# S5 mixer on one Trainium2 core: paired states for the carried product, wider products for u, one more factor in the FFN

## What is computed

```python
S5_GROUP, S5_GROUPS, S5_STATE = 16, 64, 64

def _s5_direction(u, lam_re, lam_im, log_dt, b_re, b_im, c_re, c_im, reverse):
    lam = lax.complex(lam_re, lam_im)
    dt = jnp.exp(log_dt)[:, None]
    lam_bar = jnp.exp(lam * dt)
    b_bar = ((lam_bar - 1.0) / lam)[..., None] * lax.complex(b_re, b_im)
    bu = einsum('bsgp,gnp->bsgn', u, b_bar)            # complex
    # h[t] = lam_bar * h[t-1] + bu[t], forwards or backwards over the 256 tokens
    _, hs = lax.associative_scan(combine, (a, bu), axis=1, reverse=reverse)
    return einsum('gpn,bsgn->bsgp', lax.complex(c_re, c_im), hs).real

def s5_mixer(h, ..., d_skip, w_glu):
    u = h.reshape(b, s, S5_GROUPS, S5_GROUP)
    y = (y_fwd + y_bwd).reshape(b, s, d) + d_skip * h
    g = jax.nn.gelu(y)
    val, gate = jnp.split(g @ w_glu, 2, axis=-1)
    return val * jax.nn.sigmoid(gate)
```

## Time and profile before

| what | us |
|---|---|
| median of 3 runs | 2703.33 (2701.67 to 2703.73) |
| the profiled execution | 2698.23, with a span of 2696.4 |
| PE busy | 2579.1, 96% of the span |
| DVE busy | 1822.7, 68% |
| ACT busy | 1242.6, 46% |
| POOL busy | 241.6, 9% |
| mean granted clock of PE | 0.973 |

### The profile page before, as it was taken

The page is one execution under the profiler, slowest core; times in us unless marked ns, Lnnn a source line. Parts: engine busy times, 40 slices in busy tenths (PEclk is TensorE's granted clock), DMA queues, the critical chain, the costliest instruction groups (busy, mean ns, idle before and its releaser), DMA issues.

```text
span 2696.4 us, 54054 instructions
## 1 busy us (share of the span) xinstructions
PE 2579.1 (96%) x22954; PEld 2507.2 (93%) x22954; DVE 1822.7 (68%) x2288; ACT 1242.6 (46%) x1442; POOL 241.6 (9%) x276
## 2 busy tenths in 40 slices
PE   7999849999999989999999999999999999999998
PEld 7999748999999979999999998999999999999998
DVE  5887865656566657556557557976557557986655
ACT  5334404334566644335334336575334334665433
POOL 5300140002000000000000000510000000330000
PEclk9999858999999999999999999999999999999999
DMA  5553004554676745553554554434555554443453
GB/s 205 190 186 106 18 18 157 188 187 158 187 165 151 162 93 197 187 178 140 184 184 178 187 187 151 148 127 160 190 184 185 187 187 150 158 148 141 174 187 123
DMA packets 65837, 430.73 MB, mean 160 GB/s; under 512 B 8288, under 2 KB 11360, under 8 KB 15904
## 3 DMA queue, kind: packets, MB, share of 16 engines
q1 hardware_dynamic: 58864, 410.30, 41.9%
q0 software_dynamic: 6000, 17.46, 5.2%
q10 hardware_dynamic: 832, 0.92, 0.1%
HBM read 426.45 MB, written 1.15 MB: 159 GB/s over the span
## 4 chain that ended last, share of the span: by engine, by line
PE 90%; DVE 6%; ACT 2%; issue 1%; DMA 0%; DVEq 0%; ACTq 0%
PE psum L1865 26%; PE psum L1866 26%; PE psum L1867 25%; PE psum L2187 1%; PE psum L2063 1%; DVE w_lo L1271 1%; PE psum L1898 1%; ACT w_hi L818 1%; PE psum L2163 1%; PE psum L2175 1%; PE psum L2024 1%; PE psum L1967 1%; PE psum L2033 1%; PE psum L1991 1%; PE psum L2166 1%
## 5 line engine op out<-in xcount | busy, mean ns | idle before, releaser
L1865 PE MATMUL psum<-h_hi,w_hi 128*128 128x256 f32 x4320 | 1220.7, 283 | 24.7 <-DVE h_lo L1309 14.9
L1866 PE MATMUL psum<-h_lo,w_hi 128*128 128x256 f32 x4320 | 1211.2, 280 | 0.0
L1867 PE MATMUL psum<-h_hi,w_lo 128*128 128x256 f32 x4320 | 1210.9, 280 | 0.0
L818 ACT ACTIVATE w_hi<-raw 128x2048 fp32r<-128x2048 f32 x387 | 740.3, 1914 | 907.5 <-PE psum L1867 907.5
L1271 DVE TENSOR_TENSOR w_lo<-raw,w_hi 128x2048 fp32r<-128x2048 f32 x387 | 889.4, 2299 | 376.4 <-ACT w_hi L818 376.2
L1865 PEld LDWEIGHTS psum<-h_hi,w_hi 128*128 128x128 f32 x4320 | 815.7, 189 | 35.9 <-issue 28.7
L1866 PEld LDWEIGHTS psum<-h_lo,w_hi 128*128 128x128 f32 x4320 | 816.0, 189 | 1.2 <-issue 1.0
L1867 PEld LDWEIGHTS psum<-h_hi,w_lo 128*128 128x128 f32 x4320 | 814.9, 189 | 0.0
L1865 PE MATMUL psum<-act_hi,w_hi 128*128 128x256 f32 x1536 | 429.9, 280 | 1.7 <-DVE w_lo L1271 1.0
L1866 PE MATMUL psum<-act_lo,w_hi 128*128 128x256 f32 x1536 | 429.3, 279 | 0.0
L1867 PE MATMUL psum<-act_hi,w_lo 128*128 128x256 f32 x1536 | 429.1, 279 | 0.0
(11 more groups left out here) (316 smaller groups left out, 2552.9 us busy)
## 6 DMA issues: line engine op xcount, KB each, us to landing
raw<-in_panels SPq DMA_DIRECT2D x387, 1024.0 KB, 4.8
arena<-bias_by_distance POOLq DMA_DIRECT2D x32, 384.0 KB, 7.8
x<-in_x SPq DMA_DIRECT2D x1, 1024.0 KB, 5.9
arena<-in_s_cbd POOLq DMA_DIRECT2D x4, 256.0 KB, 3.2
arena<-in_s_b SPq DMA_DIRECT2D x1, 1024.0 KB, 15.4
arena<-in_s_c SPq DMA_DIRECT2D x1, 1024.0 KB, 17.2
hidden<-in_s_cbd POOLq DMA_DIRECT2D x4, 256.0 KB, 3.3
arena<-arena POOLq DMA_DIRECT2D x32, 32.0 KB, 1.9
```

The lines of the kernel that those rows point to most:

```text
L818: a.activation(w_hi[:, s, :], raw[:, s, :], ACT.Copy).then_inc(hi_ready, 1)
L1865: t.matmul(o, w[0], xin[0], start=start, stop=False, skip_group_check=True)
L1866: t.matmul(o, w[0], xin[1], start=False, stop=False, skip_group_check=True)
L1867: return t.matmul(o, w[1], xin[0], start=False, stop=stop, skip_group_check=True)
```

## The change

- `carried(n, f)` takes one matmul for a pair where it took two: all 128 rows of W, 64 outputs, and 64 columns that come from `s5.zbd`, a buffer that holds the lower group's 31 states in the lower partitions at the left and the upper group's in the upper partitions at the right, with zeros elsewhere. ACT sets the two buffers to zero once and, after the scan, fills one for every f with 4 copies of 64 partitions by 248 elements (`s5_spread`). `carried` waits for the 4 copies, and the copies of turn n wait until `carried` of turn n - 2 is done.
- `within(f)` makes two matmuls of 64 output channels where it made one of 128. `rows_of_u` takes all eight channel tiles at once, 256 columns a matmul, in half as many.
- DVE makes all of its five W ahead of the scan; POOL waits for them (`s5_w_ready`), since it now uses DVE's temporary. Tiles run through `carried` as 0, 1, 2, 3, 6, 7, 4, 5. All four copies to `s5.y` go to DVE.
- `S5_EARLY` is 6: the FFN ahead of S5 has 12 more operations of DVE. In that FFN the copy to `act_hi` goes from DVE to ACT.
- POOL makes the powers in three rounds (powers 2; 3 and 4; 5 to 8) instead of seven.

```diff
@@ places
-        s5.w = [s5_factor(v) for v in (held[2], slot[6], slot[2], slot[5], b_flat, slot[3], slot[4], held[0])]
+        s5.w = [s5_factor(v) for v in (held[2], slot[6], slot[2], held[0], b_flat, slot[3], slot[4], slot[5])]
+        s5.zbd = hidden_flat.rearrange("p (b r c n) -> p b r c n", b=2, r=2, c=NC)
-        S5_EARLY = 5
+        S5_EARLY = 6
-        W_ORDER = (0, 1, 2, 3, 4, 6, 5, 7)
+        W_ORDER = (0, 1, 2, 3, 6, 7, 4, 5)
@@ sync: panels
                     if n == s5_n0 + 3:
-                        sp.wait_ge(s5_out_ready, W_ORDER.index(7) + 1)
+                        sp.wait_ge(s5_out_ready, W_ORDER.index(3) + 1)
@@ gpsimd
-                for k in range(2, S5_T + 1):
-                    then(tt(t0, p[:, 0, k - 1], p[:, 0, 1], ALU.mult), tt(t1, p[:, 1, k - 1], p[:, 1, 1], ALU.mult),
-                         tt(t2, p[:, 0, k - 1], p[:, 1, 1], ALU.mult), tt(t3, p[:, 1, k - 1], p[:, 0, 1], ALU.mult))
-                    then(tt(p[:, 0, k], t0, t1, ALU.subtract), tt(p[:, 1, k], t2, t3, ALU.add))
+                for k in (1, 2, 4):
+                    f0, f1 = (p[:, r, k].unsqueeze(1).to_broadcast([P, k, S5_G]) for r in range(2))
+                    lo, hi = slice(1, k + 1), slice(k + 1, 2 * k + 1)
+                    then(tt(q0, p[:, 0, lo], f0, ALU.mult), tt(q1, p[:, 1, lo], f1, ALU.mult),
+                         tt(q2, p[:, 0, lo], f1, ALU.mult), tt(q3, p[:, 1, lo], f0, ALU.mult))
+                    then(tt(p[:, 0, hi], q0, q1, ALU.subtract), tt(p[:, 1, hi], q2, q3, ALU.add))
...
+                pool.wait_ge(s5_w_ready, len(W_DVE))
@@ scalar: ffn
+                def high(c, i=None):
+                    if st["s5_follows"]:
+                        a.wait_ge(act_ready, f * FFC + c + 1 if i is None else i * 2 + f * FFC + c + 1)
+                        a.activation(act_hi[:, c % 2], act[:, c % 2], ACT.Copy).then_inc(act_hi_ready, 1)
@@ scalar: s5_mixer
+                for b in range(2):
+                    a.activation(s5.zbd[:, b].rearrange("p r c n -> p (r c) n"), zeros[:, 0:2 * S5_C].bitcast(F32).unsqueeze(
+                        1).to_broadcast([P, 2 * NC, 2 * S5_C]), ACT.Copy).then_inc(s5_zeroed, 1)
...
+                a.wait_ge(s5_step, 2 + 4 * (S5_C - 2))
+                for n, f in enumerate(W_ORDER):
+                    if n >= 2:
+                        a.wait_ge(s5_out_ready, n - 1)
+                    for d in range(2):
+                        for e in range(2):
+                            half = slice(e * S5_N, (e + 1) * S5_N)
+                            z = s5.z[half, :, f * NC + 4 * d:f * NC + 4 * d + 4, :]
+                            at = e * S5_C + 1 - d
+                            a.activation(s5.zbd[half, n % 2, :, 4 * d:4 * d + 4, at:at + S5_C - 1],
+                                         z[:, :, :, 0:S5_C - 1] if d == 0 else z[:, :, :, S5_C - 2::-1],
+                                         ACT.Copy).then_inc(s5_spread, 1)
@@ vector
-                    steps(ahead, 2)
+                    steps(ahead, 3)
...
-                due = s5_v(5)
+                due = s5_w(0)
...
-                for f, k in ((1, 4), (2, 5), (6, 6)):
+                for f, k in ((1, 4), (2, 5), (6, 6), (7, 7)):
@@ tensor
-                        t.matmul(s5_y_bank(f, g % 2)[:, at:at + S5_C], s5.tc[:, g].rearrange("p i m -> p (i m)"),
+                        for up in range(2):
+                            t.matmul(s5_y_at(f, g, 1)[half[up]], s5.tc[:, g, 4 * up:4 * up + 4].rearrange("p i m -> p (i m)"),
...
-                                    for e in range(2):
-                                        z = s5.z[half[e], r, f * NC + 4 * d + pair]
-                                        last = t.matmul(s5_y_bank(f, e)[half[up], at:at + S5_C - 1],
-                                                        s5.w[f][half[e], r, 4 * d + pair, half[up]],
+                                    last = t.matmul(s5_y_at(f, 2 * pair, 2)[half[up]], s5.w[f][:, r, 4 * d + pair, half[up]],
+                                                    s5.zbd[:, n % 2, r, 4 * d + pair, :],
```

More of the change, by code:

```diff
@@ L111, in build @@
         stages = stages[:stop]
-    for st, after in zip(stages, stages[1:] + [{}]):
+    for n, (st, after) in enumerate(zip(stages, stages[1:] + [{}])):
         st["next"] = after if after.get("late") else None
+        st["s5_follows"] = [q["kind"] for q in stages[n + 1:n + 3]] == ["norm", "s5"]
     final = stages[-1]["kind"] == "final"
@@ L879, in ffn @@
                         split(p + 4, i, 6)
+                        high(c, i)
                 split(n0 + 34)
@@ L1850, in _ @@
             for n, st in enumerate(stages):
-                st["s5_follows"] = [q["kind"] for q in stages[n + 1:n + 3]] == ["norm", "s5"]
                 todo[st["kind"]](st)
@@ L2088, in s5_mixer @@
                 t.wait_ge(s5_loaded, 64)
-                for v in range(2):
-                    t.wait_ge(h_ready, 4 * st["whole"] + 2 * v + 2)
-                    rows_of_u(v)
+                t.wait_ge(h_ready, 4 * st["whole"] + 4)
+                rows_of_u()
                 t.wait_ge(s5_u_copied, 4)
```

71 lines of the change are left out of this document (36 added, 35 removed).

## The result

| | median, us | range | executions |
|---|---|---|---|
| before | 2701.73 | 2684.08 to 2707.15 | 14 |
| changed | 2684.49 | 2660.88 to 2692.26 | 14 |

The ratio is 0.9937, with a 95% interval of 0.9916 to 0.9959: the changed kernel is faster by 17 us, between 11 and 23. The forecast was 11.5 us less than before, 2692 us with a range of 2681 to 2706. The measured median lies 7.5 us under it; 1.6 us of that is the median before, which was 2703.33 with 3 executions and is 2701.73 with 14. The profiled execution took 2680.71 us with a span of 2678.9, against 2698.23 and 2696.4.

The account below looks back on a forecast made before the run. PE bounds the kernel where it waits (for DVE's scan) or runs at a clock of 0.50. Terms -8.6 + 1.4 - 6.3 + 0 + 0 + 2.0 = -11.5 us took the median 2703.3 to 2692 us; range 2681 to 2706.

Parts of the forecast that it names:

- columns don't count: Turning u: a 32x32 instruction of 256 columns would cost 25 ns, like one of 128, so 3.2 us in all.
- POOL's preparation: FFN ahead of S5: large operations start about 10 us earlier and hold up DVE's three sums; plus 2 us.
- u: Turning u ahead of the scan: 128 instructions instead of 256, minus 3.2 us, counted within the scan's start.
- Within: Products within chunks ahead of the scan: 0.9 us less a tile, 7.3 us for PE over eight.
- The start of the scan: DVE's six products V 6 to W 7 become late instead of PE; scan at 319.5, not 328.1: minus 8.6 us.
- Spreading: Between scan and carried: ACT's four copies delay PE once, plus 1.4 us; hidden for the other seven tiles.
- Carried: Carried products: 512 instructions at 77 then 42 ns, clock back after some 6.5 us; 24.5 us, minus 6.3.
- the cheap case: Rival: 64 columns cost 56 and 31 ns like 32, GLU starts at full clock; 2683 us, chance 0.2.
- Behind carried: Last copy to `s5.y`, turn, skip and GLU: 0, with a bound of minus 3.1 us.
- The FFN: FFN ahead of S5: DVE's 12 more operations, 7.7 us, fit in its 16.1 us of waits for `w_hi`; nothing.
- The clock's rival: Rival: clock stays at 0.50 through carried, 39.4 us, plus 8.6; 2707 us in all, chance 0.15.
- the third rival: Rival: the front gives less, as u gains nothing or POOL's collision costs 5 us; 2695 to 2698 us, chance 0.15.

Follow-up runs that it names:

- e1: Changed kernel, with POOL's seven large operations waiting for DVE's three sums of squares; the sum ahead of S5 starts at 247.96 us instead of 252.44.
- e6: Changed kernel, with u's products as before (256 instructions of 128 columns in two halves); scan 77.2 us behind the sum ahead of S5, against 73.7.
- e12: Changed kernel, with two weight panel loads held until y's last turn; GLU 146.1 us behind the sum ahead of S5, against 147.0; next FFN's sum 204.6 in both.
- e8: Changed kernel, with `within` as before (one 128x128 matmul a group); scan 78.2 us behind the sum ahead of S5, against 73.7.
- e7: Changed kernel, with W 7 made behind the scan again and used last; scan 68.6 us behind the sum ahead of S5, against 73.7.
- e10: Changed kernel, with carried products cut from 64 to 32 columns, two copies a tile, part of the sum missing; 52 ns at 0.50, 26 at 1.00.
- e3: Changed kernel, with its FFN part undone (five factors V, hidden layer's upper part on DVE); scan 74.8 us behind the sum ahead of S5, against 73.7.
- e4: Kernel before, plus 28 PE products of zeros at the scan's end; next FFN's sum 219.0 us behind the sum ahead of S5, against 222.7.

## Why the prediction was right, and where not

The direction and the size held, and so did the mechanisms that were named, but for the rule "columns don't count" for u; three prices were off by much. By its own steps:

- **POOL's preparation, +2, measured +4.5.** The mechanism is the one named: the large operations at 62 meet the three sums, and the 0.99 us wait goes. The size was wrong, "1 to 2 us each, say 3 in all": the three sums grew by 4.4 us, near the upper bound of 5. The row that I had, a split that went from 2.29 to 4.50 us, said a factor of two; the factor for the sums is 2.8 (6.77 to 2.42). And a term was missing: the clock that falls behind a wait of this length, 1.55 us. e1 takes both away.
- **u, -3.2, measured -1.7 (e6: -2.1).** The step that failed is "columns don't count". A 32x32 instruction of 256 columns takes 4.63 / 128 = 36 ns, of 128 columns 23, and the row at 0.50 that I leaned on, 22 ns, was of another product, the turn of y. That one takes 1.90 us / 128 = 15 ns at a clock of 1.00 (e6, e12), so its price did go with the clock.
- **Within, -0.9 a tile, right**: 0.95 us a tile, and PE's turn of the loop 6.70 (279.10 to 285.80 in the trace) against 6.8 expected. That the gain is mostly lost at the scan was right too.
- **The start of the scan, -8.6, measured -6.5.** The switch from PE to DVE, the chain of six products behind `lags(2)` and their 46 us (46.8 measured) were right. The chain started 26.9 us behind the sum where 25.2 was expected, by u's missing 1.5 us. e8 shows PE's side of the switch, e7 the other: without W 7 in the chain, the scan waits for ACT again.
- **Spreading, +1.4, measured +2.0** (scan to carried 42.7 before, 44.8 after): a copy takes 0.43 us a step, above the row of 240 elements, below that of 512. For the other seven tiles I had given ACT 2.0 us at least; at full clock a tile lasts 1.7, and ACT holds PE up by some tenths of a microsecond in each.
- **Carried, -6.3, measured -11.6.** The clock's part was right: 0.50 for 5.6 us (6.5 expected), then 1.00. The price was the failed step. I interpolated between 32 and 128 columns, 77 and 42 ns, where the floors of 56 and 31 hold, even a little less: 53 and 26. That was the cheap case, with 18.8 us for the stretch, 19.2 measured. The page "TensorEngine Tiling (Array Packing)" of the Trainium skill says in Instruction Overhead that one column costs what sixty cost; e10, with 32 columns against 64, fits it (52 and 53 ns, 26 and 26).
- **Behind carried, 0, measured about -0.7 in the turn and -1.3 in the GLU.** The clock fell again at 397.5, as the fall behind u suggested, but came back 4.5 us into the GLU instead of 6.2.
- **The FFN, 0, right** by e3: its waits for `w_hi` took it all.

So errors of +2.5, +2.1 and +0.6 stood against -5.3, -0.7 and -1.3, and left a sum that is 2.1 us off. That it is so close is luck: terms that were too good and terms that were too bad cancelled. The clock's rival didn't occur. Of the third rival the POOL half came true, and of the cheap case the price of `carried`, though not the GLU at full clock.

What the forecast didn't say: it gave the gain in `carried` to two causes, half of the instructions and the clock. At an equal clock and without stalls the wide form is hardly cheaper (1.7 against 1.9 us a tile, 3.4 against 3.5). What I didn't see is what the count does through the stalls: they are 2.0 of the 30.8 us before (1.40, 0.21 and 0.38 in the trace), and in e4 they ate all that the high clock gave. As an estimate, at 0.50 to its end the new form would have taken 512 x 53 ns = 27.1 us, 3.7 less than before; the other 7.9 of the 11.6 us then came with the clock. The old form, given a high clock, lost it; why is open.

## What to carry over

When PE's clock is down in a stretch, first ask what a form does to the clock, and only then what it does to the count: halving the instructions by filling the rows made a tile hardly cheaper at an equal clock, and most of the 11.6 us came with the clock. Then count the stalls too, since a form with twice the instructions may be starved just when the clock is high. When work is moved ahead of a barrier, look up which engine leads there by then: W 7 was put on the very engine that had become late, and 5 us came back by moving it behind. And when a background job gets shorter, look at what it now meets: a start 10 us earlier cost 4.5 us, a third of it by the clock that fell while PE waited.

## What the runs showed of the hardware

- A 128x64 product of 32 or of 64 float32 columns takes the same: 52 and 53 ns a PE instruction at a granted clock of 0.50, 26 and 26 at 1.00. A 64x64 one of 31 columns takes 27 and 15, but at 1.00 it ran so for 171 and for 128 instructions only, with stalls of 1.27 and 2.77 us behind them.
- Old products and turns (64x64 and 32x32) didn't bring the clock back in 34.2 us before, nor in 24 us behind the stall in e4; 128x64 ones with 64 columns did in 3.7 to 6.0 us, in nine profiles.
- A wait of PE of 4.49 us was followed by about 3 us at a granted clock of 0.50, at a price of 1.55 us; behind a wait of 0.32 us the clock stayed at 1.00.
- Three DVE sums on 128x1024 took 6.77 us beside POOL operations of the same size, 2.42 and 2.41 without; POOL's own pair took 5.74 us beside DVE's splits, 4.81 beside the sums.
- The same FFN at a granted clock of 1.00 with PE never idle took 174.6 us once and 181.4 otherwise. The trace shows no cause, and it is over a third of the difference between the two profiled executions.
- PE stood for 1.23 to 1.51 us with no releaser in the turn of y, after 453 of the small products in a row; with the two 1 MB panels moved away it was 0.68 us, in one profile. What these stalls are stays open.
